# A hybrid decoder block on one core: the cross-attention's memory keys and values are made in the state-space stage and handed over through DRAM

## The reference

```python
def memory_cross_attention(h, mem_n, w_q, w_kv, g_q, g_k, w_o):
    q = (h @ w_q).reshape(bsz, seq, XA_HEADS, XA_HEAD_DIM)       # 4 heads x 128
    kv = mem_n @ w_kv                                            # 256 memory rows
    k, v = kv[..., :XA_WIDTH], kv[..., XA_WIDTH:]                # 512 columns each
    q = rmsnorm(q, g_q); k = rmsnorm(k, g_k)                     # per head
    p = softmax(q k^T * XA_HEAD_DIM ** -0.5)
    return (p v) @ w_o

x = x + concat(RMSNorm(s5_mixer(u)), RMSNorm(stick_breaking(q, k, v))) @ w_out
x = x + memory_cross_attention(rmsnorm(x, g_xa), rmsnorm(mem, g_mem), ...)
x = x + square(relu(rmsnorm(x, g_mlp) @ w_up)) @ w_down
```

## Time and profile before

| | us |
|---|---|
| runs: median of 3 (lowest to highest) | 3224.66 (3219.37 to 3226.94) |
| the profiled execution, its own time | 3229.37 |
| its span | 3227.5 |
| TensorE (PE) busy / VectorE (DVE) / ScalarE (ACT) | 2929.5 / 1679.3 / 1382.9 |
| state-space stage, first DMA issue to the next stage's loads | 440.5 to about 648 |
| cross-attention, first DMA issue to the next stage's first | 1478.1 to 1844.9 |

### The profile page before, as it was taken

How to read it: one execution, slowest core, us unless ns; L and a number is a source line. 1 busy time by engine, 2 the same in 40 slices (tenths; PEclk the granted TensorE clock), 3 DMA queues, 4 the chain that set the end, 5 groups by cost and what they waited for, 6 DMA issues and landing times. The chain is left out here.

```text
span 3227.5 us, 42824 instructions
## 1 busy us (share of the span) xinstructions
PE 2929.5 (91%) x15427; PEld 2478.3 (77%) x15427; DVE 1679.3 (52%) x2574; ACT 1382.9 (43%) x2302; POOL 691.5 (21%) x525
## 2 busy tenths in 40 slices
PE   6999945789999977995899779999999999999999
PEld 5888833578989876774788668887888788888887
DVE  5324238667878764544565475657555432234222
ACT  4333314566767663312344355556555422233221
POOL 1222112545555541310000023333322000000000
PEclk9999977989999988997999989999999999999999
DMA  4332251292223114414122234333333543354332
GB/s 159 87 92 77 75 90 22 59 222 53 54 57 78 32 34 114 121 65 176 66 79 91 97 112 131 111 107 101 107 104 118 200 148 121 122 175 169 119 109 100
DMA packets 288910, 335.21 MB, mean 104 GB/s; under 512 B 112216, under 2 KB 185952, under 8 KB 288736
## 3 DMA queue, kind: packets, MB, share of 16 engines
q1 hardware_dynamic: 288752, 333.12, 34.7%
HBM read 239.60 MB, written 92.28 MB: 103 GB/s over the span
## 5 line engine op out<-in xcount | busy, mean ns | idle before, releaser
L2944 DVE TENSOR_TENSOR f_big<-f_h_raw,f_big 128x512 fp32r<-128x512 f32 x256 | 177.2, 692 | 463.2 <-ACT f_big L2783 463.2
L2783 ACT ACTIVATE f_big<-f_h_raw 128x512 fp32r<-128x512 f32 x256 | 161.7, 632 | 498.0 <-PE f_ps_bank L3029 260.0
L2986 PE MATMUL f_ps_bank<-f_big 128*128 128x512 f32 x896 | 354.3, 395 | 19.7 <-DVE f_big L2813 8.4
L2987 PE MATMUL f_ps_bank<-f_big 128*128 128x512 f32 x896 | 352.0, 393 | 0.0
L2988 PE MATMUL f_ps_bank<-f_big 128*128 128x512 f32 x896 | 351.8, 393 | 0.0
L705 POOL TENSOR_TENSOR a_w<-a_on,a_left 128x640 f32<-128x640 f32 (+5 forms) x192 | 282.1, 1469 | 247.7 <-DVE a_left L755 109.6
L845 PE MATMUL a_ps_y<-a_wt,a_v 128*96 128x128 f32 x2176 | 270.5, 274 | 4.4 <-DVE a_yt L778 4.4
L845 PEld LDWEIGHTS a_ps_y<-a_wt,a_v 128*96 128x96 f32 x2176 | 249.5, 164 | 5.0 <-issue 5.0
L755 DVE TENSOR_TENSOR_SCAN a_left<-a_ps_z,a_one 128x896 f32<-128x896 f32 (+7 forms) x128 | 207.3, 1620 | 72.2 <-ACT a_ps_z L717 70.8
L716 ACT ACTIVATE a_on<-a_ps_z 128x640 f32<-128x640 f32 (+5 forms) x192 | 149.0, 776 | 155.4 <-PE a_ps_z L816 113.6
L2986 PEld LDWEIGHTS f_ps_bank<-f_big 128*128 128x128 f32 x896 | 170.3, 190 | 58.8 <-issue 16.8
(11 more groups left out here) (385 smaller groups left out, 6508.5 us busy)
## 6 DMA issues: line engine op xcount, KB each, us to landing
f_h_raw<-a SPq DMA_DIRECT2D x128, 512.0 KB, 3.5
f_w_raw<-in_w_up SPq DMA_DIRECT2D x32, 1024.0 KB, 7.0
a<-f_xr SPq DMA_DIRECT2D x128, 256.0 KB, 3.4
f_w_raw<-in_w_down SPq DMA_DIRECT2D x32, 512.0 KB, 3.7
p_xt<-in_x SPq DMA_DIRECT2D x16, 512.0 KB, 4.7
q<-p_qt SPq DMA_DIRECT2D x16, 512.0 KB, 3.2
k<-p_qt SPq DMA_DIRECT2D x16, 512.0 KB, 3.2
n_xt<-in_x SPq DMA_DIRECT2D x16, 512.0 KB, 4.0
```

Of the source, the lines that this page charges most:

```text
L2783: act.activation(a_slot(n, 0), a_raw(m)[:, n % 2, :], ACT.Copy).then_inc(a_high, 1)
L2944: dve.tensor_tensor(a_slot(n, 1), a_raw(n // 2)[:, n % 2, :], a_slot(n, 0).bitcast(F32), ALU.subtract).then_inc(a_low, 1)
L2986: pe.matmul(o, wv(i, 0)[:, k, :], hv(i, 0)[:, k, :], start=(k == 0), stop=False)
L2987: pe.matmul(o, wv(i, 0)[:, k, :], hv(i, 1)[:, k, :], start=False, stop=False)
```

## The change

The memory's keys and values move to the state-space stage's set-up, in other arithmetic. There, `mem` is loaded ahead of the parameters; `g_mem`, `g_q`, `g_k` and the whole of w_kv are loaded behind them, and w_kv lies in buffers that the set-up fills only later (`mat_in`, `mat_within`); `mem`, its transpose, the keys and the values lie in the buffer of `u`. ACT squares, scales, copies and normalises; PE turns the memory and makes the products with plain float32 operands, one matmul for each of 2 row tiles x 8 slices x 2 halves; the keys and values are stored to two new DRAM tensors `kt` and `mv`. The loads of `u` come behind that store. In the cross-attention the memory's work and the splits of w_kv are gone; two loads bring `kt` and `v`, and SP's order of loads is another one. The three-pass products of w_q and w_o stay.

```diff
@@ ssm_scan
+        u_flat = u[:, :, :, :].rearrange("p s g n -> p (s g n)")
+        mt = u_flat[:, 0:2048].rearrange("p (j f) -> p j f", j=MT)
+        memt = u_flat[:, 2048:4096].rearrange("p (k m) -> p k m", k=KC)
+        kt = u_flat[:, 4096:5120].rearrange("p (h m) -> p h m", h=H)
+        mv = u_flat[:, 5120:6144].rearrange("p (j f) -> p j f", j=MT)
+        k_raw = mat_in[:, :, :].rearrange("p (k a) s -> p k (a s)", k=KC)
+        v_raw = mat_within[:, :, :].rearrange("p (k a) s -> p k (a s)", k=KC)
...
         def _(sp):
+            for j in range(MT):
+                sp.dma_start(mt[:, j, :], mem[j * P:(j + 1) * P, :]).then_inc(mem_in, DMA)
...
+            sp.dma_start(gm_raw[:, :], g_mem.rearrange("(k p) -> k p", p=P)).then_inc(gm_in, DMA)
+            for n, src in enumerate((g_q, g_k)):
+                sp.dma_start(gains[:, n:n + 1], src.rearrange("(p a) -> p a", a=1)).then_inc(gm_in, DMA)
+            for half, (dst, done) in enumerate(((k_raw, keys_in), (v_raw, values_in))):
...
+            sp.wait_ge(kv_copied, 4)
+            sp.dma_start(kt_dram, kt).then_inc(kv_stored, DMA)
+            sp.dma_start(mv_dram, mv).then_inc(kv_stored, DMA)
+            sp.wait_ge(kv_stored, 2 * DMA)
             for slab in range(US):
                 load_u(slab)
...
+            pool.wait_ge(values_made, MT)
             pool.memset(mat_within[:, :, :], 0.0).then_inc(cleared, 1)
...
         def _(act):
+            act.wait_ge(mem_in, MT * DMA)
...
+                act.activation(k_junk, mt[:, j, :], ACT.Square, accum_out=mstat[:, 0, j:j + 1]).then_inc(mem_squared, 1)
+            act.wait_ge(mem_scaled, 1)
+            for j in range(MT):
+                act.activation(mt[:, j, :], mt[:, j, :], ACT.Copy, scale=mstat[:, 2, j:j + 1]).then_inc(mem_normed, 1)
+            act.wait_ge(gm_turned, 1)
+            act.activation(gm_col[:, :], o_ps[0][:, 0:KC], ACT.Copy).then_inc(gm_copied, 1)
...
+                for k in range(KC):
+                    act.activation(memt[:, k, j * P:(j + 1) * P], turned_mem[j][k // 4][:, k % 4 * P:(k % 4 + 1) * P], ACT.Copy,
+                                   scale=gm_col[:, k:k + 1]).then_inc(mem_copied, 1)
             act.wait_ge(angles, 1)
             act.activation(num[:, 6, :], num[:, 5, :], ACT.Sin).then_inc(sines, 1)
...
+            for i in range(MT * H):
+                act.wait_ge(keys_made, i // H + 1)
...
+            act.wait_ge(keys_scaled, 1)
+            for i in range(MT * H):
+                act.activation(kn[:, i, :], key_ps[i // H][:, i % H * XA_HEAD:(i % H + 1) * XA_HEAD], ACT.Copy,
+                               scale=kstat[:, 2, i:i + 1]).then_inc(keys_normed, 1)
+            for j in range(MT):
+                act.wait_ge(values_made, j + 1)
+                act.activation(mv[:, j, :], value_ps[j][:, :], ACT.Copy).then_inc(kv_copied, 1)
+            act.wait_ge(keys_turned, 1)
...
             for n in range(G // 4):
                 copy_in(n)
...
+            dve.wait_ge(mem_squared, MT)
+            rsqrt_mean(dve, link, mstat[:, 0, :], D_MODEL, mstat[:, 1, :], mstat[:, 2, :], mstat[:, 3, :])
+            dve.sem_inc(mem_scaled, 1)
             dve.wait_ge(params_in, 12 * DMA)
...
             dve.tensor_tensor(t_in, t_in, wide4, ALU.add).then_inc(in_rows, 1)
+            dve.wait_ge(gm_in, 3 * DMA)
+            link(dve.tensor_tensor(gains[:, 2:3], gains[:, 0:1], gains[:, 1:2], ALU.mult))
+            dve.wait_ge(keys_squared, MT * H)
+            rsqrt_mean(dve, link, kstat[:, 0, :], XA_HEAD, kstat[:, 1, :], kstat[:, 2, :], kstat[:, 3, :])
+            dve.sem_inc(keys_scaled, 1)
...
+            pe.wait_ge(mem_copied, MT * KC)
+            pe.wait_ge(keys_in, KC // 2 * DMA)
+            for j in range(MT):
+                for k in range(KC):
+                    mm = pe.matmul(key_ps[j][:, :], memt[:, k, j * P:(j + 1) * P], k_raw[:, k, :], start=(k == 0), stop=(k == KC - 1))
...
             pe.wait_ge(in_rows, 1)
+            pe.wait_ge(kv_copied, 4)
@@ cross_attention
-        PIECES = ([("kv", 0, k) for k in TWOS] + [("q", 0, k) for k in TWOS] + [("kv", 1, k) for k in TWOS]
-                  + [("o", 0, k) for k in range(H)])
+        PIECES = [("q", k) for k in TWOS] + [("o", k) for k in range(H)]
...
+            load_x(0)
+            sp.dma_start(g_row[:, :], g_xa.partition_broadcast(P)).then_inc(params_in, DMA)
+            load_x(1)
+            for n in range(NP):
                 sp.dma_start(raw(n), w_piece(n)[0]).then_inc(w_loaded[n % RAW], DMA)
+            load_x(2)
+            sp.dma_start(kt[:, :, :], kt_dram).then_inc(kv_in, DMA)
+            sp.dma_start(v[:, :, :], mv_dram).then_inc(kv_in, DMA)
+            load_x(3)
+            for n in range(NP, 2 * NP):
+                sp.wait_ge(w_split, n - RAW + 1)
+                sp.dma_start(raw(n), w_piece(n)[0]).then_inc(w_loaded[n % RAW], DMA)
+            load_xr(0)
+            load_xr(1)
+            load_x(4)
...
-            pipeline(act, stage, (3, 3), {-2: prepare_q, -1: square_keys, 1: prepare_v_and_o})
+            pipeline(act, stage, (3, 3), {-2: prepare_q, 0: prepare_o})
...
-            dve.wait_ge(params_in, 4 * DMA)
+            dve.wait_ge(params_in, DMA)
...
-            pipeline(dve, stage, (2, 2), {-1: prepare_q, 0: norm_keys, 1: prepare_v_k_and_o}, link)
+            pipeline(dve, stage, (2, 2), {-1: prepare_q, 1: prepare_o}, link)
...
-            pipeline(pe, stage, (1, 2), {0: await_w_q, 1: turn_keys_and_make_values, 2: await_values_and_w_o})
+            pipeline(pe, stage, (1, 2), {0: await_w_q, 1: await_keys, 2: await_w_o})
```

More of the change, by code:

```diff
@@ L857, in _, with ssm_scan @@
                     gather(m - GATHER_LAG)
-def ssm_scan(nc, a_re, a_im, log_dt, b_re, b_im, c_re, c_im, u_dram, y_dram):
+def ssm_scan(nc, a_re, a_im, log_dt, b_re, b_im, c_re, c_im, u_dram, y_dram, mem, g_mem, w_kv, g_q, g_k, kt_dram, mv_dram):
     PC = SSM_STATE
@@ L868, in ssm_scan @@
     US, TS, VS, SS, RS = 3, 4, 3, 3, 3
+    MT = MEM // P
+    H = XA_HEADS
     with ExitStack() as ctx:
@@ L1845, in _, with cross_attention @@
             body(STEPS - 1, False)
-def cross_attention(nc, x1_dram, mem, g_xa, g_mem, w_q, w_kv, g_q, g_k, w_o, x2_dram, x2_sums):
+def cross_attention(nc, x1_dram, kt_dram, mv_dram, g_xa, w_q, w_o, x2_dram, x2_sums):
     TILES = 4
```

213 lines of the change are left out of this document (82 added, 131 removed).

## The result

The changed kernel takes 3193.89 us, the median of 4 runs (3187.18 to 3197.57), beside 3224.23 for the kernel before (4 runs). The ratio is 0.9906, with a 95% interval of 0.9889 to 0.9923: 30 us faster. The forecast was 3192, between 3182 and 3208.

What follows compares the result with a forecast made beforehand. PE was taken as near full except at stage starts, where it waits on loads and DVE's chain. Terms -37.8+1.7+2.7+0.3 = -33.1 turned the profiled 3229.37 into 3196.3, or 3192 us on the median; range 3182 to 3208.

Steps and rivals of the forecast that it cites:

- The cross-attention's start: Cross-attention: tile 0's query product at S+20.3, tile 1's at S+35.1 (S the stage's first issue); gain 37.8 us.
- The second cold start: Cross-attention, tile 1's query product: PE starts at low clock after a wait of some 7 us; 2.2 us charged.
- the first cold start: Cross-attention, tile 0's query product: about 2.3 us lost to low clock, but 7.6 us taken against the old 7.4.
- `mem` ahead of the parameters: State-space set-up: loading mem first delays the parameters and so DVE; 1.7 us, between bounds 0.8 and 3.5.
- The root on DVE: State-space set-up: the keys' reciprocal root between in_rows and mat_out, on DVE's chain; costs 2.7 us.
- The memset, taken as 0: State-space set-up: POOL's 3.51 us memset moves beside mat_out's two-input operations; costs 0, with 2.1 kept for the range.
- the row of `s_sin`: Profile row: s_sin takes 690 ns alone, 1448 beside a POOL operation reading SBUF; would charge the memset 2.1 us.
- The chain of the store and `u`: State-space set-up: keys' store, u's loads, make_v and last copy of crossed meet low_ready; costs 0.3 us more.
- Rival A: Set-up's chain of memory, products, store, u and make_v is the bound, without slack; 3197 or 3212 us; chance 0.16.
- The products: State-space set-up: PE's 32 plain products at 0.86 us plus cold start, 29.7 us, fit PE's 35.89 us gap.
- Rival C: State-space set-up: plain products at half clock with uncovered weight loads take 71 us; 3233 us, slower; chance 0.02.

Runs made afterwards that it cites:

- e5: Changed kernel plus 11 useless plain products filling PE's waits ahead of the cross-attention's query products of tiles 0 and 1; 3189.34 us, ratio 0.9895.
- e7: Changed kernel with the keys' root and the small copy into mat_out moved on DVE ahead of mat_out_j's last product, so ahead of the memset; 3192.86 us, set-up 110.91.
- e9: Changed kernel plus 13 useless plain products on PE ahead of each of tile 0's and tile 1's query products; cross-attention 339.81 us against 329.46.
- e3: As e7, but the three Newton steps of the keys' root run on POOL instead of DVE; 3206.87 us, set-up 124.25.
- e2: Changed kernel with only the keys' root moved on DVE ahead of mat_out_j's last product; set-up 111.95 us, state-space stage 207.71 against 211.33.

## Why the prediction was right

- **The cross-attention's start.** Forecast S+20.3, S+35.1, and a gain of 37.8; measured S+19.6, S+34.2 and 37.7. The 0.7 of the first came from w_q, which was split at S+12.5 instead of S+13.1. Tile 0's product took 7.3 us to the turn behind it (forecast 7.6), DVE's chain the 7.3 that I had taken as 7.2. The second cold start cost 2.6 instead of 2.2: tile 1's product took 8.4 us (1516.86 to 1525.25) where 24 passes of 0.23 are 5.5 and the old one took 5.8. Some of the agreement is cancelling: tile 1 started 41.0 us earlier, not 40.0, and besides the 2.6 another 0.7 was lost on the way to the stage's end, which I have not followed. One reading of the forecast was right by luck. It charged almost nothing for the first cold start, because the old product of tile 0 "too began with a long pass (0.47)". That pass is no sign of a low clock: e5's first passes take 0.47 as well, at 2.4 GHz. But the old product went cold later on (timeline of PE before):

```profile
1521.31 0.63 PE L2260 MATMUL x_ps_q<-x_wq_lo,x_ht_hi 128*128 128x512 f32 x1
```

Its passes were 0.43 apart from 1520.88 to 1523.87, at a granted clock of 0.50. That is why 7.2 us before and 7.3 now hardly differ. Where the gain comes from the forecast left open; the passes put back show that PE's own work is 10 to 14 of it and the waits 24 to 27.
- **`mem` ahead of the parameters.** Taken as 1.7, between the issues and the bytes; it is 0.73 (14.37 to 15.10) in the pair of profiles that the table compares, and some 0.4 in the mean of all of them, which spread by 1 us. This term was mis-sized: the issues explain all of it, and no cost of the bytes shows.
- **The root on DVE.** Forecast 2.7. Without the block, L1320 to the end of the root takes 2.6 to 2.7. Right.
- **The memset, taken as 0.** This is the step that failed: "POOL's memset of 3.51 us moves from DVE's idle time to beside `mat_out`'s two-input operations". It does not. PE's products began 23.4 us after the stage's first issue and not 25.5, ended at 52.8, and the memset fell on the keys' root, 0.11 us ahead of the shift. The forecast's own times had it there as well: products to 496, and DVE at the root for 2.7 us from about 494. There it cost 3.3 us, nearly its whole length, where the range had carried 2.1. For the operations that I had in mind the 0 is right: in e7 4.43 and 4.42 beside the memset. By the row of `s_sin` the memset would have cost them 2.1; by the Trainium skill's page ("SBUF — State Buffer", section "Who interferes with whom") nothing, and these rows agree with the page. The same section of the Trainium skill says which DVE operations a POOL instruction can block altogether: copies and operations with a scalar, in a mode that uses both of DVE's port pairs. This case's runs agree, with 3.44 and 3.48 for the root's operations with scalars and 3.83 for the copy. It stands beside the rule that I used and would have named the danger: three operations with scalars and a copy lay within 6 us of the memset's start. The root's nine other steps have two tensor inputs, and in e9, where seven of them lay beside the memset, all stayed at 0.17. The 2.1 of the range came from reading the row of `s_sin` as a loss in proportion to POOL's time. Fifteen of the sixteen times POOL's `s_s_cos` starts 0.36 us ahead of DVE's `s_sin`; the sixteenth time DVE starts first (timeline of DVE and POOL before):

```profile
546.26 1.27 POOL L1028 TENSOR_TENSOR s_s_cos<-s_tables,s_sigma 128x510 f32<-128x510 f32 x1 [1.80 <-DVE s_sigma L1308]
546.62 1.46 DVE L1316 TENSOR_TENSOR s_s_sin<-s_tables,s_sigma 128x510 f32<-128x510 f32 x1
...
634.70 0.69 DVE L1316 TENSOR_TENSOR s_s_sin<-s_tables,s_sigma 128x510 f32<-128x510 f32 x1
634.79 1.71 POOL L1028 TENSOR_TENSOR s_s_cos<-s_tables,s_sigma 128x510 f32<-128x510 f32 x1 [1.85 <-issue]
```

The one that starts first keeps its length, 1.27 and 0.69, and the other ends 0.55 and 1.11 us behind it. The second is held until about the end of the first, as POOL's small operations are in e3.
- **The chain of the store and `u`.** Forecast 0.3 on top of DVE's 4.4; with DVE 6.7 late and keys copied at 64.0 it still met `low_ready` within half a us (538.87 plus 0.60 against 539.36). Counted from the stage's first issue, the store and `make_v` came 2.6 us later than forecast, because the keys' scaling waits for the same root. Both chains hang on that root, which is why e2 shortens the set-up by 2.3 and e7 by 3.3 at once. Rival A was close: 5.3 us of room in e2, none in the changed kernel. In the kernels in which ACT waits for `low_ready`, it starts 3.3 us after DVE's last `low` step (L1368 in the changed kernel). By that count the chain of the store and `u` came last by 0.3 us in the changed kernel and by 1.1 in its second profile.
- **The products.** 32 of 0.86 and a cold start, 29.7 forecast, 29.4 measured. Rival C falls with it (its limit of 62.6 us is 62.8 by its own terms, 29.7 and 33.1), and half as many again show what lies beyond.
- **The number.** -37.7 and +6.2 are -31.5, where the forecast had -33.1; the medians moved by 30.3. That 3192 and 3193.89 lie so close owes something to chance: the median of the changed kernel was 3191.42 in another series, and its set-up is not always the same. In four executions of the same set-up code (the changed kernel twice, and the two kernels that differ from it in the cross-attention alone) the state-space stage took 211.33, 212.04, 210.65 and 207.39. In the last the shift came 0.61 us before the memset and escaped (0.17), and only the copy was held (2.08), as DVE's and POOL's timeline in e9 shows:

```profile
492.03 0.17 DVE L94 TENSOR_SCALAR s_kstat<-s_kstat 128x8 int32<-128x8 int32 x1
...
492.64 3.51 POOL L1064 MEMSET s_mat_within<- 128x4096 f32 x1 [50.90 <-PE s_ps_y L1454]
...
494.36 2.08 DVE L1328 COPY s_mat_out<-s_cc 128x512 f32<-128x512 f32 x1
```

## What to carry to other kernels

Work that depends on no earlier stage is cheapest where an engine waits for another one. What it costs is what it puts on the chain that this engine waits for, so count that first: here a dozen short operations on DVE cost 2.7 us, and 29 us of products on PE, through the chain of the store and `u`, 0.3 to 1.1. A clear on POOL belongs beside DVE's two-input products, not beside short copies and operations with a scalar, which waited for its end. POOL operations that read SBUF are another case: the small ones of e3 waited for DVE's products, so they belong where DVE has none. When two chains end together, look for the step that both pass through before moving either.
